# Expert rows paced by marks, a longer ring, and half the gather scratch in a fused GDN + attention + PEER layer

## The chip, the cores and the metric

One core of a Trainium2 chip runs the kernel. The metric is device time in microseconds (us), lower is better. Time before: 3784.18 us, the median of 3 runs (3781.4 to 3789.92).

## What is computed

One layer over 1024 tokens of width 1024, all in float32. A projection feeds two token mixers, a gated delta rule in chunks (branch A) and forgetting attention (branch B). They are merged, projected, added and normed to h1. Then the PEER block picks, for each token, 8 heads x 16 = 128 experts out of 16384 and adds their output:

```
scores = q . keys            # 8 heads, 2 sides, 128 keys each
expert, gate = top 16 of the sums of two top 16 lists, softmax
u  = u_tab[expert];  act = gelu(h . u) * gate      # 128 rows of 4 KB per token
vv = v_tab[expert];  y   = sum_k act_k * vv_k      # 128 more rows of 4 KB per token
out = LayerNorm(alpha * h1 + y)
```

## The kernel before, in words

**Blocks and units.** The tokens are worked in three blocks of 2, 3 and 3 tiles of 128 tokens (`TILES`). `order()` writes out one list of 509 work units, and every engine goes through this list in order. After block 0's first expert list the list holds, for block 1: the delta rule (`prod`, `lev`, `wu`, `ws`, `o`), attention in 24 steps (`att`, `ato`), `ot`, the merge (`mix`, `wo`, `ln`), and the choice of experts (`top`, `cand`, `sel`, `idx`) with block 2's projections (`conv`, `z`, `fqk`, `fv`) in between. Then the same for block 2, whose choice has no projections beside it. After unit 509 only expert rows are left.

**Rows.** The expert work rides along. A *u row* is one gather on GpSimd's queue (L846, 128 tokens x one expert each, 4 KB per partition) and one multiply-and-sum on VectorE (L1327, "dot"). There are 128 per tile, 1024 in all. A *v row* is one gather (L860, 128 experts of one token) and a share in matmuls on TensorE: four v rows make a *quad* (L1639, 16 matmul records in the trace). There are 128 per tile too, 1024 in all, so 2048 gathers of 512 KB. A tile's v rows need all its 128 dots, and for block 0 both kinds are there before block 1's attention.

**Pace.** `pace()` gives for every unit how many dots (`DOTS`) and v rows (`TOKS`) are to be done after it. Each engine does a unit's own work and then the unit's rows: VectorE the dots of the unit, TensorE its quads. A row that has not arrived holds up its engine and all that is behind it there. GpSimd issues the gathers in the same order, ahead of their use, as long as a place is free. A u gather also waits for the dot 12 before it (`NU`), the first v gather of a quad for the quad 6 before it (`NQ`).

**Places.** Rows land in `ring`, 15 places (`NR`) of 4 KB per partition. Once block 2's scores are running, 11 more places in the arena are used too (`NX`). A place is free again when its dot or its quad is done (`place_free`). `HELD` names rows whose dot reads the token tile from PSUM; other dots before the last two tiles read it from `h_cur` in SBUF.

Of the kernel before, what the change touches and what calls it, by code (L numbers as in the profile page):

```python
# [12 lines left out]
P = 128  # L13
KB = D // P
NT = SEQ // P
TILES = [2, 3, 3]
NB = len(TILES)
FROM = [sum(TILES[:b]) for b in range(NB + 1)]
WIDTH = [P * n for n in TILES]
START = [P * n for n in FROM]  # L20
# [13 lines left out]
STEPS = [FH * n for n in TILES]  # L34
BEFORE_STEPS = [sum(STEPS[:b]) for b in range(NB)]
ARENA = 18464
NR = 15
NX = 11
NU, NQ = 12, 6
PHASE = 4  # L40
LAG = 8

SECOND, VSECOND = 192, 96
WHEN = 0.5
NCAND = 2 * TOPK // 2 + (TOPK - 1) * TOPK // 2

# [69 lines left out]
UNITS = order()  # L117
# [10 lines left out]
def share(kind, b):  # L128
    if b == 0 and kind in ("top", "cand", "sel"):
        return SHARE[kind] / 2  # L130
    return SHARE[kind] * (1.0 + 0.7 * b if kind in ("att", "ato") else 1.0)

def phase_step(toks, n, f):

    return next(s for s in range(len(toks)) if toks[s] >= P * n + 4 * PHASE * (f - 1)) + 1

def pace():

    first = UNITS.index(("idx", 0, 0))
    last = UNITS.index(("idx", NB - 1, 0))
    alone = UNITS.index(("top", NB - 1, 0))
    until = alone + round(WHEN * (last - alone))
    total = sum(share(kind, b) for kind, b, i in UNITS[first + 1:until])

    second = UNITS.index(("att", 1, 0))
    levels = sum(share(kind, b) for kind, b, i in UNITS[first + 1:second])
    dots, toks = [0], [0]
    ready, run, lately = 0, 0.0, 0  # L150
    for n, (kind, b, i) in enumerate(UNITS):

        if kind == "sel":
            ready, lately = START[b] + TOPK * i, 0
        if kind == "idx":
            ready = START[b + 1] if b else P * (i + 1)
        lately += 1
        if n <= first:
            want = max(0, ready - TOPK) + round(TOPK * lately / 7) if ready else 0
        else:  # L160

            run += share(kind, b) if n < until else 0.0
            if n < second:
                want = P + round((SECOND - P) * run / levels)
            else:
                want = SECOND + round((START[NB - 1] - SECOND) * (run - levels) / (total - levels))
        dots.append(max(dots[-1], min(want, ready, dots[-1] + 8)))
    while dots[-1] < P * NT:
        dots.append(min(P * NT, dots[-1] + 4))
    dots += [P * NT] * 56  # L170
    opened = next(s for s in range(len(dots)) if dots[s] >= P) + 1
    for s in range(1, len(dots)):
        edge = P * (toks[-1] // P + 1)
        ready = dots[s] - P - LAG if dots[s] < P * NT else toks[-1] + 4
        step = 4
        if alone < s <= last + 1:

            begin = toks[alone]
            ready, step = min(dots[s] - P - LAG if dots[s] < START[NB - 1] else P * NT, begin + round((START[NB - 1] - begin) * (s - alone) / (last + 1 - alone))), 8
        if s <= second:  # L180
            ready = VSECOND * (s - opened) // (second - opened) if s > opened else 0
        elif dots[s] < START[1]:
            ready = VSECOND + (P - LAG - VSECOND) * max(0, dots[s] - SECOND) // (START[1] - SECOND)
        if toks[-1] % P == 0 and (dots[max(0, s - 3)] < edge or toks[max(0, s - 3)] < toks[-1]):
            ready = toks[-1]
        toks.append(max(toks[-1], min(ready // 4 * 4, edge, toks[-1] + step)))
    assert toks[-1] == P * NT and toks[-5] == P * NT
    dotted = [next(s for s in range(len(dots)) if dots[s] >= P * (n + 1)) for n in range(NT)]
    begun = [next(s for s in range(len(toks)) if toks[s] > P * n) for n in range(NT)]
    summed = [next(s for s in range(len(toks)) if toks[s] >= P * (n + 1)) for n in range(NT)]  # L190
    for n in range(NT):
        for f in range(2, 32 // PHASE):
            assert phase_step(toks, n, f) < next(s for s in range(len(toks)) if toks[s] > P * n + 4 * PHASE * f)
    fetch = []
    for n in range(NT):
        stored = UNITS.index(("sel", BLOCK[n], 0)) + 1
        late = next(s for s in range(len(dots)) if dots[s] >= P * (n - 1) + 64) if n else 0
        fetch.append(max(stored, late))
    for n in range(NT):
        assert begun[n] > dotted[n] and (n == 0 or begun[n] > summed[n - 1])  # L200
        assert n < 3 or fetch[n] >= summed[n - 3] + 2
        assert fetch[n] <= next(s for s in range(len(dots)) if dots[s] > P * n)

    place, upos, vpos = 0, [], []
    for s in range(1, len(dots)):
        du, dv = dots[s] - dots[s - 1], toks[s] - toks[s - 1]
        assert du + dv <= NR
        for i in range(max(du, dv)):
            if i < du:
                upos.append(place)  # L210
                place += 1
            if i < dv:
                vpos.append(place)
                place += 1
    return dots, toks, dotted, begun, summed, fetch, upos, vpos

DOTS, TOKS, DOTTED, BEGUN, SUMMED, FETCH, UPOS, VPOS = pace()

U_AT, V_AT = {p: k for k, p in enumerate(UPOS)}, {p: k for k, p in enumerate(VPOS)}  # L220

def slots():
# [3 lines left out]
    wide = min([UPOS[k] for k in range(DOTS[begin], P * NT)] + [VPOS[k] for k in range(TOKS[begin], P * NT)])  # L227
    turns, slot, before, held = list(range(NR)), [], [], {}
    for p in range(len(at)):
        if p == wide:  # L230
            turns = list(range(NR, NR + NX)) + turns
        n = turns.pop(0)
# [72 lines left out]
def build(nc, x, xT, w_qkv, w_z, w_sm, w_fqk, w_fv, w_mix, w_out, w_pq, conv_w, bias96, alog96,  # L305
          norm_w, ln, eu, ev, out):
    ctx = ExitStack()
    with ctx:
        def sb(name, shape, dt=F32):
            return ctx.enter_context(nc.sbuf_tensor(name, shape, dt))  # L310
# [42 lines left out]

        ring = sb("ring", [P, NR, D])
        h_cur = sb("h_cur", [P, 3, D])
# [166 lines left out]
        def place(p):  # L522

            if SLOT[p] < NR:
                return ring[:, SLOT[p], :]
            return arena[:, 1536 + D * (SLOT[p] - NR):1536 + D * (SLOT[p] - NR + 1)]

# [1552 lines left out]
```

How the kernel before makes its waits and increments, by code:

```python
            def sm_(b, i):  # L569
                sp.wait_ge(s_proj, projected(b, "sm", 0))
                next_items(b, 0, 1)
# [1 line left out]
            def conv(b, c):  # L573
                if c < 12:
                    sp.wait_ge(s_proj, projected(b, "conv", c))
                    next_items(b, 1 + c, 1)
                if b == 0 and c in (9, 11):
                    fetch("gt", (c - 9) // 2)
                if c == (3 if b else 9):
                    sp.wait_ge(s_rows, b + 1)
                    sp.dma_start(d_rows[:, START[b]:START[b + 1]], rows[b]).then_inc(s_rowst, 16)
# [1 line left out]
            def z(b, i):  # L584
                sp.wait_ge(s_proj, projected(b, "z", i))
                next_items(b, 13 + 2 * i, 2)
# [1 line left out]
            def fqk(b, c):  # L588
                sp.wait_ge(s_proj, projected(b, "fqk", c))
                next_items(b, 17 + c, 1)
# [7 lines left out]
            def rT(b, i):  # L598
                if b == 0:
                    sp.wait_ge(s_rowst, 16)
                    gates(0)
# [4 lines left out]
            def nrm(b, i):  # L606
                if b:
                    sp.wait_ge(s_rowst, 16 * (b + 1))
                    sp.wait_ge(s_scr, PH * b + 1)
                    gates(FROM[b])
                    sp.wait_ge(s_ixT, transposed(FROM[b - 1]))
                    sp.wait_ge(s_zst, 48 * b)
                    chunk_of_z(b, 0)
# [1 line left out]
            def gt(b, m):  # L615
# [1 line left out]
                if m == 0:  # L617
                    for j in range(2):
                        sp.wait_ge(s_silu[j], 6)
                    for n in range(KB):
```

## Time and profile before

| | before |
|---|---|
| median of 3 runs | 3784.18 us |
| the profiled execution, own time | 3781.73 us |
| its span, first to last instruction | 3780.0 us |
| TensorE / VectorE / GpSimd busy | 2443.0 / 2085.7 / 2133.5 us |
| bytes moved, mean rate | 1251.31 MB, 331 GB/s |
| mean granted TensorE clock | 0.804 |

The profile has one execution. "Busy" of GpSimd is almost only the making of gathers. A window row gives, for a stretch, each engine's busy time with its count of instructions, the granted TensorE clock (1.00 is 2.4 GHz, 0.50 is 1.2 GHz), the share of time in which the 16 DMA engines were moving data, and the rate.

### The profile page before, as it was taken

The numbers are of one execution on the slowest core, as the hardware profiler recorded it, in microseconds if no ns is written. First come the engines' busy times: TensorE is split into PE (matmuls) and PEld (weight loads), VectorE is DVE, ScalarE is ACT, GpSimd is POOL, SyncE is SP. The second block draws the span as 40 slices with busy tenths as digits, with TensorE's granted clock in tenths as the row PEclk, the third lists the DMA queues.
The fourth block names the chain that finished last, engine by engine and source line by source line (L and its number), as shares of the span: only waits on it lengthen the run. The fifth ranks groups of instructions, "written<-read, shape, count | busy, mean of one in ns | idle before, by whom it ended". The sixth has DMA issues, their size and how long they took to land.

```text
span 3780.0 us, 34675 instructions
## 1 busy us (share of the span) xinstructions
PE 2443.0 (65%) x11152; PEld 1303.3 (34%) x11152; DVE 2085.7 (55%) x4840; ACT 596.1 (16%) x1491; POOL 2133.5 (56%) x2093
## 2 busy tenths in 40 slices
PE   8898996666799788664666779976610333333354
PEld 6686663444455434322333445433200000000010
DVE  5134888776512775757544552579688544554300
ACT  3331322322210222002222220011000000000000
POOL 1000566667600264657767774566777777677774
PEclk9899998887799889887888789987855555566678
DMA  5324899899933597989999998998999999999998
GB/s 171 99 70 163 333 365 330 326 362 399 317 116 121 197 366 287 373 335 374 406 396 383 373 388 313 344 373 327 405 410 409 410 409 410 409 410 409 409 410 336
DMA packets 358557, 1251.31 MB, mean 331 GB/s; under 512 B 39092, under 2 KB 64476, under 8 KB 354660
## 3 DMA queue, kind: packets, MB, share of 16 engines
q0 software_dynamic: 294912, 1073.87, 73.3%
q1 hardware_dynamic: 56264, 159.49, 12.2%
q10 hardware_dynamic: 7200, 15.73, 1.1%
q8 instruction: 89, 1.46, 0.2%
q14 instruction: 92, 0.75, 0.1%
HBM read 1232.82 MB, written 16.12 MB: 330 GB/s over the span
## 4 chain that ended last, share of the span: by engine, by line
PE 30%; DMA 19%; issue 18%; POOL 16%; DVE 13%; ACT 2%; DVEq 2%; ACTq 0%; POOLq 0%; SPq 0%
PE banks L1650 15%; POOL ring L860 7%; DMA ring<-in_ev,idxT 6%; DMA ring<-in_eu,eidx 6%; POOL ring L846 5%; DMA arena<-in_eu,eidx 4%; DVE ring L1327 4%; PE banks L1639 3%; PE banks L1940 3%; PE banks L1660 2%; POOL arena L860 2%; PE banks L1701 2%; POOL arena L846 2%; PE banks L1855 1%; PE banks L1878 1%
## 5 line engine op out<-in xcount | busy, mean ns | idle before, releaser
L846 POOL DMA_INDIRECT ring<-in_eu,eidx x839 | 907.3, 1081 | 1109.6 <-DVE eidx L1609 587.8
L1639 PE MATMUL banks<-ring,wide 128*32 128x512 f32 x3208 | 619.7, 815 | 785.8 <-DMA ring<-in_ev,idxT 672.0
L860 POOL DMA_INDIRECT ring<-in_ev,idxT x802 | 825.0, 1029 | 348.4 <-issue 220.7
L1327 DVE CUSTOM_DVE_ANT_0 ring<-ring,h_cur 128x1024 f32<-128x1024 f32 x550 | 650.3, 1221 | 198.7 <-DMA ring<-in_eu,eidx 194.4
L1650 PE MATMUL banks<-arena,wslot 128*128 128x384 f32 (+3 forms) x2304 | 725.7, 474 | 35.0 <-issue 23.9
L1650 PEld LDWEIGHTS banks<-arena,wslot 128*128 128x128 f32 (+1 forms) x2304 | 434.0, 192 | 327.5 <-issue 71.6
L1639 PEld LDWEIGHTS banks<-ring,wide 128*32 128x32 f32 x3208 | 116.7, 134 | 1112.4 <-issue 578.0
L1327 DVE CUSTOM_DVE_ANT_0 ring<-ring,banks 128x1024 f32<-128x1024 f32 x289 | 349.5, 1219 | 270.5 <-DMA ring<-in_eu,eidx 269.2
L1639 PE MATMUL banks<-arena,wide 128*32 128x512 f32 x888 | 237.1, 887 | 245.8 <-DMA ring<-in_ev,idxT 131.8
L860 POOL DMA_INDIRECT arena<-in_ev,idxT x222 | 213.3, 961 | 79.6 <-issue 64.4
L1660 PE MATMUL banks<-arena 128*128 128x128 f32 x1408 | 206.7, 303 | 42.2 <-ACT arena L1051 26.1
L1660 PEld LDWEIGHTS banks<-arena 128*128 128x128 f32 x1408 | 194.0, 215 | 78.6 <-ACT arena L1051 33.2
L846 POOL DMA_INDIRECT arena<-in_eu,eidx x185 | 178.1, 963 | 73.4 <-issue 48.4
L1327 DVE CUSTOM_DVE_ANT_0 arena<-arena,banks 128x1024 f32<-128x1024 f32 x116 | 140.9, 1221 | 142.5 <-DMA arena<-in_eu,eidx 142.5
L1639 PEld LDWEIGHTS banks<-arena,wide 128*32 128x32 f32 x888 | 41.8, 142 | 380.5 <-issue 152.6
L1484 DVE TENSOR_REDUCE few<-banks 128x1 f32<-128x128 f32 (+6 forms) x64 | 48.5, 758 | 205.7 <-PE banks L1858 205.4
L1650 PE MATMUL banks<-ring,wslot 128*128 128x256 f32 (+1 forms) x656 | 151.1, 387 | 11.5 <-DMA wslot<-in_w_sm 7.2
L1650 PEld LDWEIGHTS banks<-ring,wslot 128*128 128x128 f32 (+1 forms) x656 | 125.0, 193 | 29.7 <-issue 12.1
L1517 DVE TENSOR_TENSOR arena<-arena,banks 128x384 f32<-128x384 f32 x32 | 16.3, 551 | 215.2 <-PE banks L1650 215.2
L1304 DVE SCALAR_TENSOR_TENSOR h_cur<-h_cur,banks 128x512 f32<-128x512 f32 x16 | 10.2, 682 | 207.4 <-PE banks L1639 207.4
L881 ACT ACTIVATE wide<-dots 128x16 f32<-128x16 f32 x64 | 13.7, 227 | 699.0 <-PE banks L1639 698.4
L1855 PE MATMUL banks<-arena 65*128 65x512 f32 (+3 forms) x160 | 83.8, 646 | 34.2 <-DMA arena<-d_fq 18.5
(313 smaller groups left out, 2747.6 us busy)
## 6 DMA issues: line engine op xcount, KB each, us to landing
wslot<-in_w_pq SPq DMA_DIRECT2D x48, 576.0 KB, 6.2
wslot<-in_w_mix SPq DMA_DIRECT2D x16, 1536.0 KB, 6.4
wslot<-in_w_qkv SPq DMA_DIRECT2D x36, 512.0 KB, 5.7
ring<-in_eu,eidx POOLq DMA_INDIRECT x839, 9.2
ring<-in_ev,idxT POOLq DMA_INDIRECT x802, 9.2
wslot<-in_w_fqk SPq DMA_DIRECT2D x24, 512.0 KB, 5.5
wslot<-in_w_out SPq DMA_DIRECT2D x5, 2048.0 KB, 8.0
wslot<-in_w_mix SPq DMA_DIRECT2D x8, 1024.0 KB, 5.1
```

Source lines behind the costliest of these rows:

```text
L846: pool.indirect_dma_start(out=place(UPOS[k]), out_offset=None, in_=eu, in_offset=bass.IndirectOffsetOnAxis(ap=eidx[:, n % HOLD, c // TOPK, ...
L860: pool.indirect_dma_start(out=place(VPOS[k]), out_offset=None, in_=ev, in_offset=bass.IndirectOffsetOnAxis(ap=idxT[:, n % HOLD, t:t + 1], ...
L1327: dve.tensor_tensor_reduce(out=row, in0=row, in1=hp[0] if held else h_cur[:, n % 3, :] if n < NT - 2 else hp[n % 2], scale=1.0, scalar=0.0 ...
L1484: dve.tensor_reduce(nm[:, r:r + 1], SB[b][r][:, 0:w], AX.X, ALU.max, negate=True).then_inc(s_sc[r], 1)
L1517: dve.tensor_tensor(mt[b][:, k, :], gates[:, k, :], B[3 * j + 1 - k][:, 0:WIDTH[b]], ALU.mult)
L1639: last = pe.matmul(BY[k][32 * j:32 * j + 32, :], wide32[:, at:at + 32], place(VPOS[4 * q + j])[:, k * 512:(k + 1) * 512], start=(m == 0), ...
L1650: last = pe.matmul(bank, w[:, k0 + k, :], rhs[:, k, :], start=(k == 0), stop=(k == nk - 1))
L1660: last = pe.matmul(bank[:, h * P:(h + 1) * P], lhs[:, h, :], rhs[:, h, :], start=start and (stop or h == 0), stop=stop and (start or h == ...
L1701: last = pe.matmul(PN[name][b][tt][:, :], xTs[b][:, k, tt * P:(tt + 1) * P], w[:, kk, :], start=(k == 0), stop=(k == KB - 1))
L1855: pe.matmul(SB[b][r][:, k0:k1], qa[b][0:FD + 1, j, qt * P:(qt + 1) * P], kh[b][0:FD + 1, i % 2, j, k0:k1], start=True, stop=(k1 < w))
L1878: last = pe.matmul(TB[b][0][:, 0:FD], pT[b][:, k, :], vh[b][:, i % 2, k, FD * j:FD * (j + 1)], start=(k == 0), stop=(k == nk - 1))
L1940: last = pe.matmul(WO[b][nh][tt][:, :], mixT[b][:, k, tt * P:(tt + 1) * P], w[k][:, 0, :], start=(k == 0), stop=(k == KB - 1))
```

## The change

Three things change. (1) `MARKS` gives dots and v rows at seven units, and `marked` spreads the rows between two marks by each unit's `SHARE` of the work. It takes the place of the old straight line (`WHEN`) for the dots and of the old "as far behind the dots as needed" for the v rows, from block 1's attention to the end of the list. (2) The ring has 17 places instead of 15.
```diff
-NR = 15
+NR = 17
-WHEN = 0.5
+MARKS = [(("att", 1, 0), 192, 96), (("att", 1, 8), 256, 128), (("top", 1, 0), 256, 236), (("idx", 1, 0), 372, 256),
+         (("att", 2, 0), 480, 344), (("top", 2, 0), 620, 484), (("idx", 2, 0), 660, 616)]
+def marked(n):
+    at = [UNITS.index(unit) for unit, _, _ in MARKS]
+    k = next(k for k in range(1, len(at)) if n <= at[k])
+    work = [sum(share(kind, b) for kind, b, i in UNITS[at[k - 1] + 1:m + 1]) for m in (n, at[k])]
+    return [MARKS[k - 1][j] + round((MARKS[k][j] - MARKS[k - 1][j]) * work[0] / work[1]) for j in (1, 2)]
 def pace():
...
         else:
-            run += share(kind, b) if n < until else 0.0
-            if n < second:
-                want = P + round((SECOND - P) * run / levels)
-            else:
-                want = SECOND + round((START[NB - 1] - SECOND) * (run - levels) / (total - levels))
+            want = marked(n)[0]
         dots.append(max(dots[-1], min(want, ready, dots[-1] + 8)))
...
         if s <= second:
             ready = VSECOND * (s - opened) // (second - opened) if s > opened else 0
-        elif dots[s] < START[1]:
-            ready = VSECOND + (P - LAG - VSECOND) * max(0, dots[s] - SECOND) // (START[1] - SECOND)
+        elif s <= last + 1:
+            ready, step = marked(s - 1)[1], 8
+        else:
+            ready = dots[s] - P - LAG if dots[s] < P * NT else toks[-1] + 4
...
-    nc = bacc.Bacc("TRN2", target_bir_lowering=False, num_devices=1)
+    nc = bacc.Bacc("TRN2", target_bir_lowering=False, num_devices=1, dynamic_dma_scratch_size=8192)
```

The order of the units stays. What `pace()` gives before and after, worked out from its formulas (rows done after the unit, u + v):

| unit | number | before | after |
|---|---|---|---|
| block 1, first attention step | 245 | 194 + 96 | 192 + 96 |
| block 1, ninth attention step | 262 | 216 + 104 | 256 + 128 |
| block 1, `ot` | 296 | 256 + 120 | 256 + 176 |
| block 1, `top` 0 (merge done) | 314 | 256 + 120 | 256 + 236 |
| block 1, `idx` (choice done) | 374 | 368 + 224 | 368 + 256 |
| block 2, first attention step | 408 | 472 + 336 | 480 + 344 |
| block 2, `top` 0 | 477 | 612 + 476 | 620 + 484 |
| block 2, `idx` (list done) | 509 | 640 + 624 | 660 + 616 |
| all rows | | 1024 + 1024 | 1024 + 1024 |

In the choice of block 1 the before version has about 16 v rows for each head, 8 of them together with the head's 16 dots; the after version has 20 v rows in the whole choice after `top` 0.

## Rows read from the trace of the kernel before

**Rows 1.** The page: DMA in 40 slices of 94.5 us, in tenths.

```profile
DMA  5324899899933597989999998998999999999998
```

**Rows 2.** VectorE in order of time: start us, us, what, [idle before].

```profile
903.43 0.56 DVE L1484 TENSOR_REDUCE few<-banks 128x1 f32<-128x384 f32 x1 [4.20 <-PE banks L1858]
...
953.71 0.82 DVE L1484 TENSOR_REDUCE few<-banks 128x1 f32<-128x640 f32 x1 [1.31 <-PE banks L1858]
...
1678.04 0.30 DVE L1553 RECIPROCAL arena<-arena 128x24 f32<-128x24 f32 x1 [7.43 <-ACT gate L1224]
...
2005.22 0.96 DVE L1484 TENSOR_REDUCE few<-banks 128x1 f32<-128x768 f32 x1 [7.77 <-PE banks L1858]
...
2716.91 0.30 DVE L1553 RECIPROCAL arena<-arena 128x24 f32<-128x24 f32 x1 [4.15 <-ACT gate L1224]
```

**Rows 3.** Windows by stage, all engines.

```profile
core 0: us, PE busy (x) PEld busy (x) DVE busy (x) ACT busy (x) POOL busy (x), PEclk, DMA share, GB/s
903.00:954.00 51.00, 38.05 (x161) 24.04 (x160) 32.65 (x56) 11.95 (x34) 39.42 (x32) 0.64 1.04 382
954.00:1056.00 102.00, 66.42 (x351) 44.23 (x349) 60.01 (x103) 28.51 (x77) 57.22 (x47) 0.75 0.84 291
1056.00:1229.00 173.00, 168.94 (x496) 93.64 (x496) 28.61 (x50) 12.66 (x26) 0.00 (x0) 0.99 0.31 113
1229.00:1678.00 449.00, 349.60 (x1295) 174.48 (x1295) 307.13 (x986) 82.51 (x230) 225.52 (x209) 0.89 0.82 308
1678.00:2005.00 327.00, 189.00 (x1147) 106.63 (x1147) 181.52 (x312) 82.25 (x184) 231.75 (x232) 0.82 1.01 392
...
2500.00:2717.00 217.00, 144.54 (x742) 64.38 (x741) 192.50 (x761) 28.34 (x99) 141.25 (x134) 0.84 0.94 363
2717.00:3780.00 1063.00, 345.25 (x1734) 63.52 (x1734) 493.95 (x809) 18.02 (x46) 765.20 (x808) 0.61 1.01 403
```

**Rows 4.** A window inside the last stretch, all engines, columns as in Rows 3.

```profile
3000.00:3400.00 400.00, 135.47 (x605) 23.54 (x609) 199.42 (x327) 6.53 (x17) 292.39 (x312) 0.55 1.03 409
```

**Rows 5.** Windows of the v matmuls (L1639) alone: PE, PEld, clock, DMA, GB/s.

```profile
954.00:1056.00 102.00, 11.09 (x64) 2.20 (x64) 0.75 0.84 291
...
1229.00:1678.00 449.00, 64.58 (x400) 12.66 (x400) 0.89 0.82 308
```

**Rows 6.** Windows of the dots (L1327) alone, two instructions a dot: DVE, clock, DMA.

```profile
954.00:1056.00 102.00, 48.22 (x82) 0.75 0.84 291
```

**Rows 7.** TensorE in order of time: block 1's merge, then block 2's.

```profile
1056.29 125.75 PE L1650 MATMUL banks<-arena,wslot 128*128 128x384 f32 x384 [0.69 <-ACT arena L1139]
...
2262.77 15.75 PE L1650 MATMUL banks<-arena,wslot 128*128 128x384 f32 x48 [0.69 <-ACT arena L1139]
2278.44 1.92 PE L1639 MATMUL banks<-ring,wide 128*32 128x512 f32 x16
2280.30 15.75 PE L1650 MATMUL banks<-arena,wslot 128*128 128x384 f32 x48
```

**Rows 8.** Waits in block 1's choice, 1229 to 1678: total us, times, longest.

```profile
DVE ring L1327 <- DMA ring<-in_eu,eidx: 95.4, 22, 17.2
POOL ring L846 <- PE banks L1639: 87.1, 9, 21.1
PE banks L1639 <- DMA ring<-in_ev,idxT: 85.8, 11, 18.3
```

**Rows 9.** GpSimd in order of time: attention, choice, last stretch.

```profile
907.99 1.98 POOL L860 DMA_INDIRECT ring<-in_ev,idxT  x1 [0.30 <-issue]
...
1502.71 0.93 POOL L846 DMA_INDIRECT ring<-in_eu,eidx  x1 [18.72 <-PE banks L1639]
...
3046.20 0.94 POOL L860 DMA_INDIRECT ring<-in_ev,idxT  x1 [0.30 <-issue]
```

**Rows 10.** The page: queue of the gathers, packets, MB, share.

```profile
q0 software_dynamic: 294912, 1073.87, 73.3%
```

More of the change, by code:

```diff
@@ L142, in pace @@
     last = UNITS.index(("idx", NB - 1, 0))
[L143 to L147, printed above, removed]
+    second = UNITS.index(MARKS[0][0])
     levels = sum(share(kind, b) for kind, b, i in UNITS[first + 1:second])
@@ L159, in pace @@
             want = max(0, ready - TOPK) + round(TOPK * lately / 7) if ready else 0
-        else:
-            run += share(kind, b) if n < until else 0.0
-            if n < second:
-                want = P + round((SECOND - P) * run / levels)
-            else:
-                want = SECOND + round((START[NB - 1] - SECOND) * (run - levels) / (total - levels))
+        elif n < second:
+            run += share(kind, b)
+            want = P + round((SECOND - P) * run / levels)
+        else:
+            want = marked(n)[0]
         dots.append(max(dots[-1], min(want, ready, dots[-1] + 8)))
@@ L173, in pace @@
         edge = P * (toks[-1] // P + 1)
-        ready = dots[s] - P - LAG if dots[s] < P * NT else toks[-1] + 4
         step = 4
-        if alone < s <= last + 1:
-            begin = toks[alone]
-            ready, step = min(dots[s] - P - LAG if dots[s] < START[NB - 1] else P * NT, begin + round((START[NB - 1] - begin) * (s - alone) / (last + 1 - alone))), 8
         if s <= second:
             ready = VSECOND * (s - opened) // (second - opened) if s > opened else 0
-        elif dots[s] < START[1]:
-            ready = VSECOND + (P - LAG - VSECOND) * max(0, dots[s] - SECOND) // (START[1] - SECOND)
+        elif s <= last + 1:
+            ready, step = marked(s - 1)[1], 8
+        else:
+            ready = dots[s] - P - LAG if dots[s] < P * NT else toks[-1] + 4
         if toks[-1] % P == 0 and (dots[max(0, s - 3)] < edge or toks[max(0, s - 3)] < toks[-1]):
```

## The prediction

> **What bounds the kernel.** I read the slices of the page first. The DMA engines are full from about 1420 us to the end and nearly full before 1040 us, but there is a hole from about 1040 to 1320 us, at 3, 3 and 5 tenths [rows 1]. The first dots of an attention step, the closing of an expert list and so on give the borders of the stages [rows 2], and the windows cut at these borders say what each stage is held by [rows 3]:
>
> - Attention of block 1, steps 1 to 8 (903 to 954): the DMA share is 1.04, and GpSimd makes gathers for 39.42 of 51 us. With the 0.30 us between two gathers [rows 9] its 32 gathers fill 49 us. This stage goes at the pace of rows.
> - Steps 9 to 24 (954 to 1056): nothing is full. TensorE 66 of 102 us, VectorE 60.
> - The merge (1056 to 1229): TensorE 169 of 173 us, and not one gather. This is the hole.
> - The choice (1229 to 1678): DMA 0.82, TensorE 350 and VectorE 307 of 449 us. The waits explain it [rows 8]: VectorE waits 95.4 us for u rows, TensorE 85.8 us for v rows, and GpSimd 87.1 us for places that unfinished quads hold. These are one circle: v rows fill the places, so u rows are late.
> - From 1678 on, levels, attention and the end all show a DMA share of 1.01 where no merge or choice runs. In the last stretch 312 gathers take 400 us, 1.28 us each [rows 4]. There a row less is 1.28 us less.
>
> So rows are dear in the last 2100 us, cheap in the merge, and what they cost in the choice is a detour over places.
>
> **The change, term by term.** The counts of rows are those of the planner's table. Times are against the profiled execution (3781.73 us, span 3780.0); the median of the runs is 2.45 us above it, which I add at the end.
>
> *Steps 1 to 8.* 64 u and 32 v rows where there were 22 and 8, so 66 more in a stage that already goes at the pace of rows. At the best DMA rate, 1.28 us a row [rows 4], that is +84. At this stage's own rate of gathers, (39.42 + 32 x 0.30) / 32 = 1.53 us [rows 3], it is +101. The second is high here because a gather made while a dot runs can take 1.98 us, where in the last stretch it takes 0.94 [rows 9]. Some ten rows are in flight at the start and need not be made in the stage, and what is in flight at its end is v rows that nobody waits for, which can take off up to 10 x 1.28 = 13. I take **+90**, bounds +71 and +101.
>
> The Trainium skill ("SBUF — State Buffer", "Who interferes with whom") speaks against packing dots and gathers together: a VectorE instruction with two inputs in SBUF and a GpSimd operation that reads SBUF lock each other out. The trace agrees, since the dots of this stage read row and token tile from SBUF, and those of the last stretch have the tile in PSUM. By that rule the term is the +101, without it the +84.
>
> *Steps 9 to 24 and `ot`.* 40 dots go and 32 v rows come (48 for 16). The dots cost VectorE 48.22 us for 41 [rows 6], in the middle of the chain scores, maximum, exponent, transposes. The eight quads cost TensorE 11.09 / 4 = 2.8 us each [rows 5], 22 us, which brings it to 88 of 102 us. VectorE falls to 12. I take **-5**, bounds -12 (half of TensorE's present idle time gone beyond the quads) and +8.
>
> *The merge.* 14 quads come (from 176 to 232 v rows; the last four rows up to 236 are done after `top` 0). TensorE is full, so they lie on the path. The same merge of block 2 already has quads between its groups: 1.92 us for 16 matmuls, of which 1.86 is added to the start of the next group, at the full clock [rows 7]. 14 x 1.86 = **+26**; at the 2.8 us of the slower clock +39. The DMA they need, 56 x 1.28 = 72 us in 173 with a share of 0.31 in use, is free.
>
> *The choice.* 80 v rows go (104 to 24), the 112 u rows stay. TensorE loses 20 quads of 64.58 / 25 = 2.6 us [rows 5], from 350 to 298. VectorE keeps its 307. With 17 places and a u lead of at most 12, a head's u rows no longer meet a ring full of v rows, so the stalls of GpSimd (18.72 us in one head [rows 9]) go and with them most of VectorE's 95.4 us. What is left: in block 2's choice, with few dots and no projections, VectorE is busy for 192.5 of 217 us [rows 3], 89%; 307 / 0.89 = 345. Taking the wait alone away gives 449 - 95 = 354. I take 351, **-98**; bounds -50 (TensorE's 298 plus the chain through ScalarE keep half) and -115.
>
> Up to the end of the list of block 1 this is +90 - 5 + 26 - 98 = **+13**, with 32 v rows more done than before.
>
> *Levels of block 2.* 200 rows instead of 216, DMA full, 327 us for 232 gathers, 1.41 each [rows 3]. 16 fewer: **-22**. If the delta rule's own chain holds the stage, 0.
>
> *Attention and merge of block 2.* 90 + 88 rows and 50 + 52 in both: 0. The rows are only 8 + 8 further on.
>
> *Choice of block 2.* 4 rows fewer, but 12 more dots at 1.18 us where VectorE is 89% busy, 14 us, partly in place of waiting. **+5**, bounds -5 and +14.
>
> *The end.* 772 rows instead of 784 at 1.28 us: **-15**.
>
> *The two places.* In the last stretch DMA is full with 26 places, so 28 only make the queue deeper. Elsewhere two more rows ahead could save stalls. 0, bounds -15 and 0.
>
> *The halved scratch.* The queue shows 294912 packets for 2048 gathers, 144 each [rows 10], so 9 for each of 16 engines. At most 28 places can be in flight. Nothing in the trace shows GpSimd held by anything but places, dots, quads and its own making of gathers. 0. If it did hold, every gather is late: each 0.1 us beyond the 1.28 us in the last 772 is +77. The Trainium skill ("Debugging Trainium Hangs", "Descriptor Overflow") names this area as one that can be overfilled, at 16 KiB a partition. With the 16-byte descriptors of its page "DMA: Bandwidth & Descriptors" ("Terms") an estimate is 8192 / 16 = 512 per engine against 28 x 9 = 252 in flight, so it would not bind.
>
> Sum: +13 - 22 + 5 - 15 = **-19**, that is 3762.7 beside the profiled run and **3765** beside the median.
>
> **Rivals.**
>
> *The choice does not shorten enough (slower).* Its heads could be held by TensorE: 285 us of its own work without quads, in order with projections that wait for ScalarE. In the window it was 78% busy with 86 us of waiting for v rows, which speaks for the forecast; VectorE's idle time that is not the u wait, 47 us, speaks for the rival. At -60 instead of -98 the sum is +19, 3803. It decides from -79 on: with less, the kernel is slower than before.
>
> *A wash.* Attention takes what the choice gives, and the levels' chain hides the 16 rows' gain: -19 + 22 = +3, 3787, within 0.2% of before. About 0.2% is also what a measurement of this kernel can tell from no change.
>
> *More than forecast.* The lead pays in attention (+76 instead of +90) and the choice goes to -113: 29 us better, 3736. For it speaks that the places held by quads were the first cause in the choice.
>
> *The scratch binds.* Above; 3840 or more. Against it: packets per gather and places.
>
> **How the numbers follow.** Forecast 0.42 (its own range 3749 to 3776), more than forecast 0.16, a wash 0.17, choice too long 0.21, scratch 0.04. So faster by over 0.2% 0.58, within 0.2% 0.17, slower 0.25. The range 3724 to 3805 leaves out about 0.05 below, and above it the scratch and half of the long choices, 0.14.
>
> **What the profile after would show.** From the first to the ninth attention step of block 1 about 140 us instead of 50, GpSimd making gathers nearly all of it, above 1.1 us each. The merge some 26 us longer, with quads of 1.9 us between its groups, TensorE still full. The two list closings of block 1 and 2 (L1553): the first 13 us later than before, the second about 4 us earlier. In the choice of block 1 the wait of u gathers for quads near zero, VectorE's wait for u rows below 20 us, the stage near 350 us. The last stretch about 15 us shorter at an unchanged 409 GB/s, gathers at 0.94 us. The prediction is wrong if the ninth step comes after 100 us or less, if the choice stays above 380 us though the waits are gone, or if gathers in the last stretch get longer.

## The result, and the profile after

The changed kernel takes 3733.2 us (median of 4 runs, 3730.22 to 3737.82) against 3784.76 for the kernel before; the ratio is 0.9864, 95% interval 0.9847 to 0.9881. That is 52 us faster where 19 were forecast, and still inside the forecast range of 3724 to 3805. The direction was right, the size was not.

The page of the changed kernel, the slices that answer to [rows 1]:

```profile
PE   8899996664479999956666889875601333333354
DMA  5324899999996658999999998987999999999998
```

The hole at 3, 3 and 5 tenths is filled to 6, 6, 5 and 8. A new shallow one has come near 2550 us (8, 7).

The windows of the changed kernel, cut at the same borders as [rows 3] (steps 1 to 8, steps 9 to 24, merge, choice, levels of block 2, then the choice of block 2 from the end of its merge, and the end):

```profile
612.00:888.00 276.00, 171.29 (x1081) 105.18 (x1082) 222.92 (x577) 86.41 (x207) 199.66 (x189) 0.83 0.98 373
888.00:1020.00 132.00, 55.60 (x238) 26.95 (x237) 77.31 (x129) 12.15 (x34) 101.93 (x86) 0.57 0.99 364
1020.00:1123.00 103.00, 76.20 (x500) 42.97 (x499) 23.84 (x40) 33.47 (x86) 61.81 (x62) 0.89 0.96 356
1123.00:1316.00 193.00, 192.99 (x704) 97.29 (x700) 29.20 (x51) 11.82 (x27) 44.64 (x47) 1.00 0.64 237
1316.00:1651.00 335.00, 299.07 (x1018) 164.85 (x1010) 298.01 (x978) 79.79 (x220) 172.67 (x132) 0.95 0.81 293
1651.00:1940.00 289.00, 177.81 (x1035) 107.89 (x1035) 188.15 (x328) 80.50 (x181) 211.26 (x207) 0.81 1.00 385
2394.00:2698.00 304.00, 188.67 (x896) 81.70 (x894) 230.57 (x860) 33.89 (x109) 191.02 (x180) 0.81 0.89 343
2698.00:3733.00 1035.00, 343.72 (x1670) 62.16 (x1670) 470.62 (x771) 17.80 (x45) 753.03 (x777) 0.63 1.01 398
```

Steps 1 to 8 of the attention take 132 us for 51, the merge 193 for 173 with TensorE full, the choice 335 for 449. The first row is one that the forecast had not looked at: the levels of block 1, whose rows the new marks do not touch. Before, they were

```profile
611.00:903.00 292.00, 179.07 (x1082) 111.23 (x1082) 224.36 (x577) 86.58 (x206) 197.81 (x189) 0.80 0.94 352
```

The same 189 gathers now take 16 us less, at a DMA share of 0.98 for 0.94.

The table has the length of each stage, from the traces of all the kernels that matter below (us; attention starts with the first L1484 of its block, merge with its first L1650, a choice ends with L1553). The levels of block 1 begin with the L1553 at 608 to 614 us.

| stage | before | 16 places | 17 places | marks, 15 | changed | no lead | merge full | dots early |
|---|---|---|---|---|---|---|---|---|
| levels 1 | 292.6 | 285.5 | 281.3 | 293.5 | 276.6 | 281.3 | 280.8 | 280.2 |
| steps 1-8 | 50.3 | 50.8 | 51.3 | 137.3 | 131.7 | 129.4 | 104.7 | 131.3 |
| steps 9-24 | 102.6 | 98.6 | 97.1 | 104.8 | 103.4 | 96.9 | 107.1 | 103.7 |
| merge 1 | 174.0 | 174.7 | 172.4 | 192.9 | 192.9 | 186.8 | 202.1 | 192.9 |
| choice 1 | 447.7 | 444.2 | 438.6 | 334.7 | 334.4 | 335.4 | 345.6 | 334.5 |
| levels 2 | 327.2 | 323.2 | 317.1 | 292.4 | 289.2 | 326.5 | 289.1 | 289.0 |
| attention, merge 2 | 446.6 | 449.5 | 447.7 | 453.6 | 454.0 | 455.8 | 452.1 | 453.0 |
| choice 2 | 265.0 | 263.3 | 260.2 | 310.5 | 303.8 | 304.4 | 305.0 | 273.3 |
| end | 1060.2 | 1063.5 | 1063.2 | 1019.8 | 1032.8 | 1016.9 | 1019.9 | 1010.2 |

### The profile page after: what moved, and what is told of

It is laid out like the page before. It is cut to its first block, busy times and chain, and to the rows that moved or that the text cites. A ratio compares the mean times of both kernels' runs of the same rounds, so it can differ in the third digit from the quotient of the medians.

```text
span 3733.5 us, 34678 instructions
## 1 busy us (share of the span) xinstructions
PE 2440.0 (65%) x11152; PEld 1293.1 (35%) x11152; DVE 2082.2 (56%) x4840; ACT 596.8 (16%) x1492; POOL 2181.7 (58%) x2093
## 4 chain that ended last, share of the span: by engine, by line
PE 31%; DVE 17%; POOL 17%; DMA 16%; issue 14%; DVEq 2%; ACT 2%; POOLq 0%; ACTq 0%; SPq 0%
PE banks L1650 15%; POOL ring L860 7%; DMA ring<-in_eu,eidx 7%; DVE ring L1327 6%; POOL ring L846 6%; DMA ring<-in_ev,idxT 6%; PE banks L1639 4%; PE banks L1940 3%; PE banks L1660 3%; POOL arena L860 2%; POOL arena L846 2%; PE banks L1701 2%; DMA arena<-in_ev,idxT 2%; DVE arena L1271 1%; PE banks L1690 1%
## 5 line engine op out<-in xcount | busy, mean ns | idle before, releaser
L846 POOL DMA_INDIRECT ring<-in_eu,eidx x858 | 961.5, 1121 | 925.0 <-DVE eidx L1609 408.1
L1639 PE MATMUL banks<-ring,wide 128*32 128x512 f32 x3264 | 630.9, 825 | 747.9 <-DMA ring<-in_ev,idxT 674.8
L860 POOL DMA_INDIRECT ring<-in_ev,idxT x816 | 842.6, 1033 | 468.0 <-issue 224.5
L1650 PE MATMUL banks<-arena,wslot 128*128 128x384 f32 (+3 forms) x2304 | 720.3, 471 | 26.3 <-issue 19.9
L1327 DVE CUSTOM_DVE_ANT_0 ring<-ring,h_cur 128x1024 f32<-128x1024 f32 x555 | 653.9, 1221 | 116.7 <-DMA ring<-in_eu,eidx 114.3
L1650 PEld LDWEIGHTS banks<-arena,wslot 128*128 128x128 f32 (+1 forms) x2304 | 431.8, 191 | 312.2 <-issue 57.1
L1327 DVE CUSTOM_DVE_ANT_0 ring<-ring,banks 128x1024 f32<-128x1024 f32 x303 | 364.6, 1219 | 255.1 <-DMA ring<-in_eu,eidx 254.0
L1639 PEld LDWEIGHTS banks<-ring,wide 128*32 128x32 f32 x3264 | 117.0, 133 | 1075.5 <-DMA ring<-in_ev,idxT 609.3
L1639 PE MATMUL banks<-arena,wide 128*32 128x512 f32 x832 | 216.2, 908 | 247.6 <-DMA ring<-in_ev,idxT 134.7
L860 POOL DMA_INDIRECT arena<-in_ev,idxT x208 | 202.7, 975 | 66.8 <-issue 58.9
L1660 PEld LDWEIGHTS banks<-arena 128*128 128x128 f32 x1408 | 192.9, 213 | 80.5 <-ACT arena L1051 34.4
L1327 DVE CUSTOM_DVE_ANT_0 arena<-arena,banks 128x1024 f32<-128x1024 f32 x109 | 132.6, 1221 | 132.8 <-DMA arena<-in_eu,eidx 132.7
L846 POOL DMA_INDIRECT arena<-in_eu,eidx x166 | 165.1, 994 | 56.3 <-issue 49.6
L1484 DVE TENSOR_REDUCE few<-banks 128x1 f32<-128x128 f32 (+6 forms) x64 | 48.5, 757 | 237.0 <-PE banks L1858 237.0
L1639 PEld LDWEIGHTS banks<-arena,wide 128*32 128x32 f32 x832 | 38.1, 142 | 387.7 <-issue 148.7
L1650 PE MATMUL banks<-ring,wslot 128*128 128x256 f32 (+1 forms) x656 | 152.0, 389 | 11.5 <-DMA wslot<-in_w_sm 7.1
L1650 PEld LDWEIGHTS banks<-ring,wslot 128*128 128x128 f32 (+1 forms) x656 | 125.9, 195 | 29.9 <-issue 12.0
L1940 PE MATMUL banks<-wslot,arena 128*128 128x512 f32 x224 | 98.3, 595 | 1.5 <-issue 1.5
```

Source lines behind the costliest of these rows:

```text
L846: pool.indirect_dma_start(out=place(UPOS[k]), out_offset=None, in_=eu, in_offset=bass.IndirectOffsetOnAxis(ap=eidx[:, n % HOLD, c // TOPK, ...
L860: pool.indirect_dma_start(out=place(VPOS[k]), out_offset=None, in_=ev, in_offset=bass.IndirectOffsetOnAxis(ap=idxT[:, n % HOLD, t:t + 1], ...
L1327: dve.tensor_tensor_reduce(out=row, in0=row, in1=hp[0] if held else h_cur[:, n % 3, :] if n < NT - 2 else hp[n % 2], scale=1.0, scalar=0.0 ...
L1484: dve.tensor_reduce(nm[:, r:r + 1], SB[b][r][:, 0:w], AX.X, ALU.max, negate=True).then_inc(s_sc[r], 1)
L1639: last = pe.matmul(BY[k][32 * j:32 * j + 32, :], wide32[:, at:at + 32], place(VPOS[4 * q + j])[:, k * 512:(k + 1) * 512], start=(m == 0), ...
L1650: last = pe.matmul(bank, w[:, k0 + k, :], rhs[:, k, :], start=(k == 0), stop=(k == nk - 1))
```

## The experiments

All ratios are to the kernel before, run on the same chip beside the experiment (medians of before from 3785 to 3790).

### The places alone

```diff
-NR = 15
+NR = 17
-    nc = bacc.Bacc("TRN2", target_bir_lowering=False, num_devices=1)
+    nc = bacc.Bacc("TRN2", target_bir_lowering=False, num_devices=1, dynamic_dma_scratch_size=8192)
```

> The kernel before with 17 places and the halved scratch, its old pace kept. Theory A (the two places pay wherever rows are late, which the first block's levels showed by ending 15 us earlier at the same row counts): levels of block 1 end 10 to 18 us earlier, the choice of block 1 about 10 us shorter, the whole 3755 to 3772 us. Theory B (my prediction: places are worth nothing, all the gain is the marks): within 5 us of 3784.

Measured: 3743.16 us, ratio 0.9879 (0.9863 to 0.9894). Two places without any new mark give nearly the whole gain, more than either theory allowed. The gain is spread: 11 us in the levels of block 1, 5 in steps 9 to 24, 9 in the choice, 10 in the levels of block 2, 5 in its choice, nothing at the end. What gave way are GpSimd's waits for places. From 611 to 2000 us, first the kernel before, then the one with 17 places:

```profile
POOL ring L846 <- PE banks L1639: 119.5, 23, 21.1
...
POOL ring L860 <- DVE dots L1327: 43.3, 26, 21.5
POOL ring L846 <- DVE dots L1327: 40.6, 19, 13.7
POOL ring L860 <- PE banks L1639: 24.9, 11, 8.0
```

```profile
POOL ring L846 <- PE banks L1639: 91.2, 18, 17.9
POOL ring L846 <- DVE dots L1327: 46.9, 19, 13.7
POOL ring L860 <- DVE dots L1327: 33.4, 24, 19.0
POOL ring L860 <- PE banks L1639: 16.1, 12, 3.3
```

Together 228 us against 188. While GpSimd waits for a place no gather is made, and soon no DMA engine has work; the levels of block 1 in this kernel:

```profile
610.00:891.00 281.00, 176.71 (x1082) 109.10 (x1082) 223.46 (x576) 86.29 (x206) 199.19 (x190) 0.81 0.97 367
```

### One place

```diff
-NR = 15
+NR = 16
-    nc = bacc.Bacc("TRN2", target_bir_lowering=False, num_devices=1)
+    nc = bacc.Bacc("TRN2", target_bir_lowering=False, num_devices=1, dynamic_dma_scratch_size=12288)
```

> The kernel before, old pace, 16 places (scratch 12288 bytes). Theory A (each place lets GpSimd run one gather further before it has to wait, in every stretch where the DMA engines are nearly full but not quite): between before and the run with 17 places, 3755 to 3772 us, again spread over levels, attention and choice. Rival (the gain is a threshold, such as a ring whose length suits the pattern of u and v rows): all of it or nothing, 3743 or 3785.

Measured: 3767.5 us, ratio 0.995 (0.9937 to 0.9962). One place gives 19 us, two give 46, in the same stages. There is no one threshold, as the rival had it; the second place gave somewhat more than the first.

### The marks alone

```diff
-NR = 17
+NR = 15
-    nc = bacc.Bacc("TRN2", target_bir_lowering=False, num_devices=1, dynamic_dma_scratch_size=8192)
+    nc = bacc.Bacc("TRN2", target_bir_lowering=False, num_devices=1)
```

> The changed kernel with 15 places and the old scratch. Theory A: the marks are worth about 30 us by themselves, 3748 to 3760 us, and the levels of block 1 take their old 292 us again. Theory B: 3733 us, as with 17 places. A third one (the marks pay only with the places): 3775 or more.

Measured: 3753.08 us, ratio 0.99 (0.9887 to 0.9913). The marks alone give 1.0%, the places alone 1.2%, both together 1.36%. That looks as if both mostly filled the same idle DMA time, but the stages do not bear it out. Up to the end of the choice of block 2 the two places save 40 us on the old pace (2106 to 2066 us by the table) and still 34 us on the marks (2120 to 2086). The two overlap in the choice of block 1 (the places give 9 us there on the old pace, none on the marks) and in the levels of block 2 (10 and 3). Another 13 us are lost in the end of the changed kernel, 1032.8 us for 1019.8, for a reason that is found further down ("More in the merge"). In the choice of block 1 the marks take away the wait for places that quads hold (with 334.7 and 334.4 us it is equally long with 15 and 17 places).

### The scratch alone

```diff
-    nc = bacc.Bacc("TRN2", target_bir_lowering=False, num_devices=1)
+    nc = bacc.Bacc("TRN2", target_bir_lowering=False, num_devices=1, dynamic_dma_scratch_size=8192)
```

> The kernel before with the halved scratch alone, 15 places. Theory A and B: 3784 us, within 0.2%, gathers at their old 0.94 us in the last stretch. Rival (the smaller descriptor area or the shifted addresses change the gathers themselves): off by more than 8 us either way, with another gather time in the last stretch.

Measured: 3788.03 us, ratio 0.9992 (0.9978 to 1.0006). NR stays at 15. The halved scratch costs nothing and gives nothing that 12 runs can show.

### 18 places, a quarter of the scratch

```diff
-NR = 17
+NR = 18
-    nc = bacc.Bacc("TRN2", target_bir_lowering=False, num_devices=1, dynamic_dma_scratch_size=8192)
+    nc = bacc.Bacc("TRN2", target_bir_lowering=False, num_devices=1, dynamic_dma_scratch_size=4096)
```

> The changed kernel with 18 places and a scratch of 4096 bytes. Theory A: a little more, 3720 to 3733 us, since the marks have already taken away most waits for places. Rival 1 (17 is enough under the marks): 3731 to 3736. Rival 2 (the scratch of 4096 bytes binds, 28 gathers by the count of packets against 29 places at the end): the last stretch is longer, 3740 or more.

Measured: 3723.02 us, ratio 0.9829 (0.9816 to 0.9842), against 0.9864 with 17. That the third place itself pays these 10 us is not shown. In the profiles nothing is saved before the end: the second list closing (L1553) comes at 2700.0 us, where it was at 2697.9. The whole difference lies in the end, 1018.9 us for 1032.8, and 1018.9 is what the end takes with the marks and 15 places too (1019.8). With 29 places there it is no longer than elsewhere, so no binding of 4096 bytes shows either.

### No v rows in the merge

```diff
-MARKS = [..., (("top", 1, 0), 256, 236), ...]
+MARKS = [..., (("mix", 1, 0), 256, 180), (("top", 1, 0), 256, 180), ...]
```

> The changed kernel with no v rows in block 1's merge: a mark holds them at 180 from the start of the merge to the first unit of the choice, and the 76 v rows up to 256 are spread over the choice. Theory A (v rows in the choice cost by holding places and keeping u rows late): the merge is 20 to 26 us shorter, back to about 173 us, the choice 336 us grows by 40 to 70, the whole 3750 to 3775 us. Rival (the choice is held by VectorE's and TensorE's own work, and the quads fit in their gaps): the choice grows by less than 20 us and the whole is 3733 us or less.

Measured: 3737.79 us, ratio 0.9862 (0.9844 to 0.988), no different from the changed kernel. The merge was 18.5 us shorter (174.4), the choice 33 us longer (367.0), which is between the two theories. The first list closing thus came 14 us later, the levels after it took the same 290 us, but the end took 1020.1 us for 1032.8. In the runs' times, to spread the rows over the merge is worth nothing that they can show. In the profiles it is worth 14 us in merge and choice, and the changed kernel loses about as much again in its end.

### 32 rows less ahead

```diff
-MARKS = [..., (("top", 1, 0), 256, 236), (("idx", 1, 0), 372, 256), ...]
+MARKS = [..., (("top", 1, 0), 256, 204), (("idx", 1, 0), 372, 224), ...]
```

> The changed kernel with 32 v rows fewer before the end of block 1's choice (224 as in the kernel before, not 256), which come back in the levels of block 2. If a row taken out of a full stretch is worth 1.28 us or more there: attention and merge of block 1 about 15 to 25 us shorter, levels of block 2 35 to 45 longer, the whole about 20 us slower, 3748 to 3760. If the levels were long only for other reasons: the levels grow by less than 20 us and the whole is 3733 or less.

Measured: 3751.69 us, ratio 0.991 (0.9896 to 0.9924). As expected by the first theory: 18 us slower than the changed kernel. Steps 9 to 24 and the merge were 13 us shorter, the levels of block 2 37 us longer (326.5, the 327.2 of before again). Its end took 1016.9 us for 1032.8, so up to the second list closing the loss is nearer to 30 us than to 18.

### Dots early in the choice of block 2

```diff
-MARKS = [..., (("top", 2, 0), 620, 484), (("idx", 2, 0), 660, 616)]
+MARKS = [..., (("top", 2, 0), 620, 484), (("sel", 2, 1), 640, 512), (("idx", 2, 0), 660, 616)]
```

> The changed kernel with one more mark, 640 dots and 512 v rows at the second head of block 2's choice, so that the v rows of the next tile start 10 units earlier instead of standing at 512 for eleven units. Theory (the standstill leaves the DMA engines idle, share 0.88 there, and makes this choice 304 us long instead of 265): choice of block 2 shorter by 15 to 30 us, the rest the same, 3705 to 3720 us. Rival (the choice is held by VectorE's work and the rows only move): within 5 us of 3733.

Measured: 3684.11 us, ratio 0.974 (0.9723 to 0.9756), 49 us below the changed kernel, more than the 3705 to 3720 of the theory. The choice of block 2 takes 273.3 us for 303.8, at the upper end of what was expected. The end, which was to stay the same, takes 1010.2 us for 1032.8. Fewer gathers are left for it (762 for 777 in the windows), and part of the rest is again the changed kernel's own slow end. A comparison without that is the same mark added with 18 places, 3676.37 for 3723.02 us, which is 47 us. First the changed kernel's window after the dip begins, then this kernel's:

```profile
2500.00:2698.00 198.00, 116.00 (x561) 45.38 (x561) 153.07 (x580) 20.57 (x73) 123.37 (x118) 0.78 0.87 331
```

```profile
2500.00:2666.00 166.00, 119.25 (x609) 49.22 (x607) 152.00 (x609) 20.70 (x76) 125.63 (x122) 0.83 1.03 409
2666.00:3679.00 1013.00, 338.23 (x1651) 60.46 (x1651) 469.51 (x771) 17.31 (x44) 721.74 (x762) 0.59 1.01 400
```

The v rows beyond 512 need all 640 dots of their tile. The changed kernel reaches 640 dots only at the fifth head, and its v rows stand at 512 for eleven units; here they stand for two, and DMA stays full through the choice.

### More in the merge, less in the attention

```diff
-MARKS = [..., (("att", 1, 8), 256, 128), (("top", 1, 0), 256, 236), ...]
+MARKS = [..., (("att", 1, 8), 256, 108), (("mix", 1, 0), 256, 156), (("top", 1, 0), 256, 240), ...]
```

> The changed kernel with 20 v rows fewer in steps 1 to 8 of block 1's attention (108 instead of 128 at the ninth step, 156 instead of 180 at the merge), which come back as six more quads in the merge. If steps 1 to 8 go at the pace of rows, each at 1.28 to 1.5 us: 26 to 30 us shorter, 102 to 106 us; merge 11 us longer at 1.86 us a quad, about 204; the whole 10 to 18 us less, 3715 to 3723. Rival (the 64 dots and u rows alone hold these steps): the steps stay above 120 us and the whole is 3733 to 3745.

Measured: 3723.95 us, ratio 0.9834 (0.9818 to 0.9851). The whole is just above the expected 3715 to 3723. The two stage prices held (104.7 and 202.1 us), but of the 27 us saved in steps 1 to 8 the merge took 9, as priced, and steps 9 to 24 and the choice another 15 (+3.7, +11.2), which was not. The second list closing is at 2697.6 us, where it was at 2697.9. What is left is in the end, 1019.9 us for 1032.8. The windows from 2698 us, first the changed kernel, then this one:

```profile
2698.00:2800.00 102.00, 8.11 (x35) 1.77 (x35) 79.95 (x131) 2.89 (x4) 80.06 (x73) 0.51 0.99 375
2800.00:2900.00 100.00, 18.21 (x80) 3.07 (x80) 62.16 (x102) 1.59 (x2) 77.59 (x74) 0.52 0.99 380
```

```profile
2698.00:2800.00 102.00, 6.44 (x38) 1.61 (x35) 87.23 (x142) 3.12 (x5) 77.93 (x80) 0.53 1.02 407
2800.00:2900.00 100.00, 22.15 (x97) 3.79 (x97) 63.72 (x106) 2.30 (x6) 75.91 (x80) 0.53 1.03 409
```

The changed kernel moves rows at 375 to 380 GB/s there, the other at 407 to 409; the first 200 us of the end run at 405 to 409 GB/s in all the other kernels too. It costs some 13 us in this profile.

The traces show what sets the slower pace. It is the making of the gathers, though the DMA share reads 0.99. GpSimd makes gather after gather in these 200 us with only the 0.30 us between two that it always has, but some gathers take longer. The gathers of u rows into the ring, up to the last dot that reads the token tile from SBUF, in the changed kernel (2698 to 2886 us) and in this one (2698 to 2868):

```profile
L846 POOL DMA_INDIRECT ring<-in_eu,eidx x66 | 71.5, 1083 | 20.1 <-issue 20.1
```

```profile
L846 POOL DMA_INDIRECT ring<-in_eu,eidx x65 | 63.1, 970 | 19.8 <-issue 19.8
```

One long gather of the changed kernel, with the dot that was running when it began, and the last dot that reads `h_cur` with the first that reads the tile from PSUM (`banks`):

```profile
2740.40 1.23 DVE L1327 CUSTOM_DVE_ANT_0 ring<-ring,h_cur 128x1024 f32<-128x1024 f32 x1 [0.65 <-DMA ring<-in_eu,eidx]
2740.87 1.57 POOL L846 DMA_INDIRECT arena<-in_eu,eidx  x1 [0.30 <-issue]
...
2884.13 1.23 DVE L1327 CUSTOM_DVE_ANT_0 ring<-ring,h_cur 128x1024 f32<-128x1024 f32 x1 [1.33 <-DMA ring<-in_eu,eidx]
...
2886.91 1.22 DVE L1327 CUSTOM_DVE_ANT_0 ring<-ring,banks 128x1024 f32<-128x1024 f32 x1 [0.88 <-DMA ring<-in_eu,eidx]
```

All gathers from 2698 to 2900 us, by how long after the start of such a dot they began, with their mean time (counted from the two traces):

| gather began | changed kernel | more in the merge |
|---|---|---|
| 0 to 0.2 us into a dot | 3, 1.92 us | 1, 1.86 us |
| 0.2 to 0.4 | 4, 1.73 | none |
| 0.4 to 0.6 | 7, 1.57 | none |
| 0.6 to 0.8 | 13, 1.33 | none |
| 0.8 to 1.0 | 14, 1.15 | 3, 1.08 |
| later | 68, 0.97 | 105, 0.98 |
| beside no such dot | 36, 0.94 | 49, 0.94 |

A gather that begins while the dot runs takes what is left of the dot's 1.23 us and some 0.9 us more. In this kernel nearly all of them begin when the dot is almost over, in the changed kernel 41 do not. From 2887 us on, with no such dot left, the changed kernel too runs at 410 GB/s. What puts the gathers out of step in the one kernel and not in the other stays open. So does whether the changed kernel's other runs have it, but it is likely: all four (3730.22 to 3737.82) lie above all five of this kernel (3720.29 to 3728.5), whose profile is equal up to the second list closing.

### The extra mark with 18 places, and all three

> The changed kernel with the extra mark of the run before (640 dots and 512 v rows at the second head of block 2's choice) and 18 places with a scratch of 4096 bytes. If the two gains are of different kinds they add: 10 us below the extra mark alone, 3671 to 3678 us. If both only fill the same idle time of the DMA engines: 3682 to 3686.

Measured: 3676.37 us, ratio 0.9711 (0.9694 to 0.9729), as expected if the two gains add. It is 8 us below the extra mark alone, but the two intervals overlap a little (0.9723 to 0.9756 there). Neither kernel has the slow stretch in its end, so this is the fairer test of a third place. It leaves a gain likely but not clear, since the two profiled executions take the same time (3680.38 and 3680.69 us).

> The changed kernel with all three: the extra mark in block 2's choice, 18 places, and the 20 v rows moved from attention into the merge. If the prices add: 3655 to 3668 us. If not, no better than the extra mark with 18 places.

Measured: 3670.46 us, ratio 0.9696 (0.9679 to 0.9713), the fastest kernel here, 3.0% below before and 63 us below the changed kernel. It missed the 3655 to 3668 by a little; against 0.9711 the moved v rows are not clear of the runs' spread.

## Why the prediction was wrong

**The step that failed** is "the two places: 0, bounds -15 and 0". Alone they measured 46 us, and on top of the marks still 0.99 to 0.9864, some 14 us (34 us up to the second list closing in the profiles, of which 13 are lost again in the end). Of the 33 us by which the forecast was low, these 14 are the places; the other 19 are terms of the marks, which follow. The step asked where DMA is full and took a full DMA as proof that more places only deepen the queue. That holds for the end, which did not change (1060.2, 1063.2). It does not hold at a DMA share of 0.94 in the levels of block 1 or 0.82 in the choice, and the waits of GpSimd for dots and quads, 228 us between 611 and 2000, were in the trace to be added up. The forecast used them in one stage only, the choice. It also never looked at the levels of block 1, since no mark touches them, although the ring runs through them.

**The marks** were forecast at -19 and measured at 0.99, which is -38 us. By stage, in the profiles of the kernel before and of the marks with 15 places:

- Steps 1 to 8: +87 for +90. The price between the two rates was right. In the changed kernel GpSimd made 86 gathers in 132 us, 1.19 us each against 0.94 in the last stretch [rows 9]; "above 1.1 us each" was seen. "Nearly all of it" was seen too: it was busy for 102 us of 132, and with the 0.30 us between two gathers, as the forecast counted, 86 gathers fill 128 us.
- Steps 9 to 24: +2 for -5.
- The merge: +19 for +26. 13 quads lie in it, not 14, and some of their 1.86 us fell into gaps; the quads look as foreseen, in order of time on TensorE in the changed kernel:

```profile
1139.34 1.92 PE L1639 MATMUL banks<-ring,wide 128*32 128x512 f32 x16
1141.20 15.75 PE L1650 MATMUL banks<-arena,wslot 128*128 128x384 f32 x48
```

- The choice of block 1: -113 for -98. The place circle was the right mechanism, and the rival that TensorE's own work would hold the heads fell. VectorE's waits in this choice of the changed kernel, against 95.4 us for u rows in [rows 8]:

```profile
DVE best L1265 <- ACT arena L1189: 17.6, 1, 17.6
DVE arena L1342 <- ACT arena L928: 1.0, 1, 1.0
DVE ring L1327 <- DMA ring<-in_eu,eidx: 0.8, 2, 0.6
```

- The levels of block 2: -35 for -22. The run with 32 rows less ahead gave it all back, 37 us for 32 rows, 1.2 us each, so 16 rows explain some 19 us. The other 16 us stay open. They could be in how the rows lie: the old pace has 8 u and 4 v rows in each of the first six units there, the new one 7 or 3 u and at first no v rows. No run tests that by itself.
- The choice of block 2: +45 for +5. This term missed what the planner's numbers already held, the standstill of the v rows at 512. The forecast looked only at VectorE.
- Attention and merge of block 2: +7 for 0.
- The end: -40 for -15. The step counted rows by the plan, 784 to 772, but GpSimd is not where the plan is when VectorE closes the list. By the gathers made after that, 808 [rows 3] to 776, 32 at 1.28 us are 41. The end with the marks and 15 places:

```profile
2730.00:3752.00 1022.00, 343.18 (x1670) 61.75 (x1670) 470.72 (x773) 17.80 (x45) 736.43 (x776) 0.59 1.01 403
```

The choice of block 2 and the end nearly cancel: +5 together, forecast at -10. The stages of the marks before them come to -33, forecast at -9. So the marks gained for the reason given, the place circle in the choice of block 1, but their total hides two terms that were off by 40 and 25 us with opposite signs, which is luck. In the profiles the marks alone are 27 us, by the ratio 38; the forecast of 19 was low by either.

**The signs that the forecast named.** The ninth attention step came after 132 us (about 140 forecast) and the choice took 334 us (about 350). The two list closings did not come as forecast, 13 us later and 4 us earlier: they came 27 and 19 us earlier, with the places' gain in them. With the marks and 15 places they came 4 us earlier and 13 us later. "If gathers in the last stretch get longer" was named as a sign of being wrong, and for the first 200 us of the last stretch they did, 1.08 us for 0.98 in the kernel before. The forecast said that the dots of the last stretch have the token tile in PSUM. That is so only from 2931 us on in the kernel before (2887 us in the changed one); until then they read it from SBUF.

**The scratch** was right at 0, shown by itself, and so is what the forecast made of it: 8192 bytes do not bind. The estimate behind it, by the 16-byte descriptors of the Trainium skill ("DMA: Bandwidth & Descriptors", "Terms"), was 512 against 252 in flight. At 4096 bytes the same estimate gives 256 against 29 x 9 = 261, so it would bind there if all places were in flight at once. No run shows it binding, and no run shows how many are in flight.

## What to carry to other kernels

Add up what the issuing engine waits for places over the whole trace before calling a buffer long enough; a DMA share of 0.94 is not full, and the first added 4 KB place here gave 0.5%, the second 0.7%. When work is moved, compute the plan's standstills from its own rule (which work must be complete before the next may start) as carefully as its totals: one extra mark against a standstill gave 47 us with 18 places, nearly as much as the whole change. Price the stage that follows a stage border by what was really issued, not by what the plan has done.

## What the hardware showed that was not expected

A DMA share of 0.99 did not mean that the DMA engines set the pace. With the same kind of transfers the changed kernel ran at 375 to 380 GB/s at that share for 200 us, and a kernel that differs only in the order of some rows over 1 ms earlier at 407 to 409. GpSimd set the pace there, at 1.08 us a gather and 0.30 us between two.

A gather beside a dot that reads both inputs from SBUF costs what is left of the dot when it begins. In the changed kernel's steps 1 to 8, 13 gathers began in the first 0.2 us of such a dot and took 1.90 us in the mean, 14 began after 1.0 us and took 0.96. At the start of the end of the kernel before, 120 of 123 began after 1.0 us, and the dots cost the gathers next to nothing. So the same dots and gathers can cost much or nothing, by how they fall into step.
